# Two-operand matmuls 512 columns wide in the gate, up and down projections, and the normed activations moved by 32 bytes in SBUF

## The reference

```python
h   = rmsnorm(x, mix_norm_w);  u = h @ w_in            # forgetting attention and Mamba-2 SSD from u
x   = x + concat(y_A, y_B) @ w_out
h   = rmsnorm(x, ffn_norm_w)
g, up = split(h @ w_gate_up)                           # 2048 -> 2 * 5632
g   = causal_dwconv3(g)
x   = x + (silu(g) * up) @ w_down                      # 5632 -> 2048
h   = rmsnorm(x, ple_norm_w)
x   = x + sigmoid(h @ w_ple_gate) * (p @ w_ple_proj)
out = rmsnorm(x, final_norm_w)
```

## Time and profile before

| | us |
|---|---|
| median of 3 runs (1280.76 to 1281.69) | 1280.86 |
| the profiled execution: its time / its span | 1281.42 / 1279.7 |
| TensorE busy / weight loads busy (they overlap) | 1267.1 / 1221.7 |
| VectorE / ScalarE / GpSimd busy | 829.0 / 604.4 / 60.7 |
| DMA | 177 GB/s, 58% of the 16 engines' span |

### The profile page before, as it was taken

One profiled execution on the slowest core, in us unless ns is written; L12 is line 12 of the kernel. 1 busy time (PEld: TensorE's weight loads), 2 busy tenths in 40 slices (PEclk: granted clock), 3 DMA queues, 4 the chain that ended last, 5 costly groups with the idle time before them and its releaser, 6 DMA issues.

```text
span 1279.7 us, 25047 instructions
## 1 busy us (share of the span) xinstructions
PE 1267.1 (99%) x9950; PEld 1221.7 (95%) x9950; DVE 829.0 (65%) x1068; ACT 604.4 (47%) x775; POOL 60.7 (5%) x66
## 2 busy tenths in 40 slices
PE   9999999999999999999999999999999999999997
PEld 7999998789999999999999999999999999999885
DVE  6698777777777576665665575666665464646554
ACT  6444555556544454444444444443444343434555
POOL 2000000001221100000000000000001010101000
PEclk9999999999999999999999999999999999999998
DMA  8566555435556566666666666666655656566652
GB/s 257 160 188 186 155 148 148 116 114 151 186 176 198 181 182 182 182 182 184 183 184 182 180 180 181 181 181 183 188 183 167 209 162 208 165 211 204 196 188 99
DMA packets 118020, 227.05 MB, mean 177 GB/s; under 512 B 7392, under 2 KB 8452, under 8 KB 117828
## 3 DMA queue, kind: packets, MB, share of 16 engines
q1 hardware_dynamic: 117860, 225.89, 58.0%
q0 software_dynamic: 96, 0.26, 0.1%
HBM read 224.03 MB, written 2.10 MB: 177 GB/s over the span
## 4 chain that ended last, share of the span: by engine, by line
PE 98%; DMA 1%; SPq 0%; ACT 0%; issue 0%; DVE 0%; ACTq 0%; DVEq 0%
PE ps L316 27%; PE ps L317 27%; PE ps L318 27%; PE ps L343 4%; PE ps L345 4%; PE ps L344 4%; DMA w_raw<-in_w_in 1%; PE ps L734 1%; PE ps L737 1%; PE ps L778 1%; PE ps L761 0%; PE ps L791 0%; PE ps L748 0%; PE ps L776 0%; PE ps L902 0%
## 5 line engine op out<-in xcount | busy, mean ns | idle before, releaser
L301 DVE TENSOR_TENSOR w_lo<-w_raw,w_hi 128x1024 fp32r<-128x1024 f32 x413 | 506.4, 1231 | 366.6 <-ACT w_hi L296 363.8
L296 ACT ACTIVATE w_hi<-w_raw 128x1024 fp32r<-128x1024 f32 x413 | 435.9, 1058 | 525.3 <-PE ps L318 484.8
L316 PE MATMUL ps<-hHi,w_hi 128*128 128x256 f32 x1984 | 564.5, 285 | 0.8 <-DVE w_lo L301 0.8
L317 PE MATMUL ps<-hLo,w_hi 128*128 128x256 f32 x1984 | 561.3, 283 | 0.0
L318 PE MATMUL ps<-hHi,w_lo 128*128 128x256 f32 x1984 | 561.3, 283 | 0.0
L316 PEld LDWEIGHTS ps<-hHi,w_hi 128*128 128x128 f32 x1984 | 380.2, 192 | 1.5 <-issue 1.4
L317 PEld LDWEIGHTS ps<-hLo,w_hi 128*128 128x128 f32 x1984 | 380.3, 192 | 0.0
L318 PEld LDWEIGHTS ps<-hHi,w_lo 128*128 128x128 f32 x1984 | 380.2, 192 | 0.0
L316 PE MATMUL ps<-actHi,w_hi 128*128 (+1 forms) x704 | 196.9, 280 | 0.0
L317 PE MATMUL ps<-actLo,w_hi 128*128 (+1 forms) x704 | 196.9, 280 | 0.0
L318 PE MATMUL ps<-actHi,w_lo 128*128 (+1 forms) x704 | 196.9, 280 | 0.0
(11 more groups left out here) (242 smaller groups left out, 969.5 us busy)
## 6 DMA issues: line engine op xcount, KB each, us to landing
w_raw<-in_w_gate_up SPq DMA_DIRECT2D x176, 512.0 KB, 4.0
w_raw<-in_w_in SPq DMA_DIRECT2D x88, 512.0 KB, 3.7
w_raw<-in_w_down SPq DMA_DIRECT2D x88, 512.0 KB, 4.8
w_raw<-in_w_out SPq DMA_DIRECT2D x32, 512.0 KB, 4.7
w_raw<-in_w_ple_gate SPq DMA_DIRECT2D x32, 512.0 KB, 4.7
w_raw<-in_w_ple_proj SPq DMA_DIRECT2D x4, 512.0 KB, 5.4
out_x<-out_tok SPq DMA_DIRECT2D x8, 256.0 KB, 3.1
xtok<-in_x SPq DMA_DIRECT2D x3, 512.0 KB, 8.8
```

Of the source, the lines that this page charges most:

```text
L296: act.activation(parts(n)[0], w_raw[:, n % RING, :], ACT.Copy).then_inc(w_hi_made, 1)
L301: dve.tensor_tensor(lo, w_raw[:, n % RING, :], hi, ALU.subtract).then_inc(w_lo_made, 1)
L316: pe.matmul(dst, hi, opHi(k), start=start and m % 2 == 0, stop=False, skip_group_check=True)
L317: pe.matmul(dst, hi, opLo(k), start=False, stop=False, skip_group_check=True)
```

## The change

- `multiply_wide`: the activation's hi and lo parts now lie side by side (`h_parts`, `act_parts`: 512 columns for each k). One matmul of 512 columns multiplies `w_hi` by both, w_hi·xHi into columns 0 to 255 of a bank and w_hi·xLo into columns 256 to 511; one of 256 columns adds w_lo·xHi to the second half. Each 128-wide output tile now fills a bank, so a step over 512 weight columns takes 4 banks instead of 2 and the two halves of PSUM hold one unit each.
- The gate and up chunks are cut otherwise: two k slices by 256 gate and 256 up columns, 8 chunks to a unit, in two DMAs of 128x512 each, in runs of 256 columns of memory (1 KB) instead of 512 (2 KB). Still 176 chunks of 512 KB.
- The two halves of a bank have to be added. ScalarE copies the second half to `sumsq` and `sq` (`ffn_unit_part`), VectorE adds, then scales by `rms` in two ops of their own; `add_down` adds each half to `xT`, 4 ops for 2.
- `STATS1_AT` goes from chunk 11 to chunk 4 of the first 8-chunk unit.
- 32 bytes of padding ahead of `h_parts` and 32 behind. In the built program `h_parts` begins 32 bytes past a multiple of 128; `w_raw`, `w_hi` and `w_lo` 64 past; the arena 96 past; `pHi` at a multiple of 128. So the distance of the arena's tiles from the weight tiles is what it was, that of h from them is now 32 bytes more or less than a multiple of 64.
- The in-projection and the token-wise groups keep their instructions and read h from `h_parts`.

```diff
-        hHi, hLo = sb("hHi", [P, KD, T], F32R), sb("hLo", [P, KD, T], F32R)
+        half_line = sb("half_line", [P, 8])
+        h_parts = sb("h_parts", [P, KD, 2, T], F32R)
+        line_rest = sb("line_rest", [P, 8])
+        hHi, hLo = h_parts[:, :, 0, :], h_parts[:, :, 1, :]
...
+        act_parts = at("act_parts", [P, FT, 2, T], F32R, 0)
+        actHi, actLo = act_parts[:, :, 0, :], act_parts[:, :, 1, :]
...
+        def load_unit_chunk(sp, n, src, q=0):
...
+            for a in range(2):
+                sp.dma_start(w_raw[:, n % RING, a * COLS:(a + 1) * COLS].rearrange("p (b c) -> p b c", b=2),
+                             src[:, a, :, :]).then_inc(w_landed[n % RING], 16)
...
+        def multiply_wide(pe, n, both_of, bank_of, first, last, q=0):
+
+            pe.wait_ge(w_lo_made, n + RING * q + 1)
+            for i in range(2 * MT):
+                k, m = divmod(i, MT)
+                both = both_of(k)
+                hi, lo = (w[:, n % RING, i * P:(i + 1) * P] for w in (w_hi, w_lo))
+                pe.matmul(ps[:, bank_of[m], :], hi, both.rearrange("p b t -> p (b t)"),
+                          start=first and k == 0, stop=False, skip_group_check=True)
+                mm = pe.matmul(ps[:, bank_of[m], T:2 * T], lo, both[:, 0, :],
+                               start=False, stop=last and k == 1, skip_group_check=True)
+            return mm.then_inc(w_used, 1)
...
-        STATS1_AT = 11
-        UNIT_AT = (3, 9)
+        STATS1_AT = 4
+        U_IN, U_TAPS, U_SILU, U_ACT, U_HI, U_LO = LEAD, LEAD + 1, LEAD + 2, LEAD + 3, LEAD + 4, LEAD + 4
...
+            def ffn_unit_part(u, half, unit_end):
+
+                act.wait_ge(w_used, unit_end)
+                act.wait_ge(ffn_out, u + 1)
+                for part, a in ((sumsq, 0), (sq, 2)):
+                    b = WIDE_BANKS[half][a]
+                    copy(part[:, :, :], ps[:, b:b + 2, T:2 * T]).then_inc(ffn_part, 1)
...
+            def add_down(g):
+
+                banks = WIDE_BANKS[g % 2]
+                for half in range(2):
+                    for b in range(2):
+                        k = MT * g + 2 * b
+                        part = ps[:, banks[2 * b]:banks[2 * b] + 2, half * T:(half + 1) * T]
...
+                        dve.tensor_tensor(xT[:, k:k + 2, :], part, xT[:, k:k + 2, :],
+                                          ALU.add).then_inc(x_new if half else x_part, 1)
```

More of the change, by code:

```diff
@@ L290, in make_hi @@
         def make_hi(act, n, q=0):
-            act.wait_ge(w_landed[n % RING], 16 * (n // RING + q + 1))
+            act.wait_ge(*landed(n, q))
             if RING <= n < n_last:
@@ L846, in ffn_chunk @@
             def ffn_chunk(n, k, half, q=0):
[L847 to L862, removed]
+                return multiply_wide(pe, n, lambda kk: h_parts[:, 2 * k + kk, :, :], WIDE_BANKS[half], k == 0, k == KU - 1, q)
+            for j in range(2):
+                for k in range(KU):
+                    if j == 0:
+                        if k == 0:
+                            for name in ("o1", "o2"):
+                                pe.wait_ge(*evacuated[name])
+                        pe.wait_ge(h_lo_made, KD + 2 * k + 2)
+                    elif k == 0:
+                        pe.wait_ge(root_made, 2)
+                        pe.wait_ge(*evacuated["o3"])
+                    ffn_chunk(n_ffn + j * KU + k, k, j)
+                    if j == 0 and k == STATS1_AT:
+                        pe.wait_ge(*evacuated["o0"])
+                        stats(1, 4, columns=False)
+            with pe.Fori(0, NU // 2 - 1) as i:
                 for j in range(2):
-                    for k in range(KD):
+                    for k in range(KU):
                         if k == 0:
-                            pe.wait_ge(ffn_out, i * 4 + (1, 3)[j])
-                        ffn_chunk(n_ffn + (1 + j) * KD + k, k, 1 - j, i * (2 * KD // RING))
+                            pe.wait_ge(ffn_out, i * 2 + (2 + j))
+                        ffn_chunk(n_ffn + (2 + j) * KU + k, k, j, i * (2 * KU // RING))
             for g in range(NDN):
@@ L1103, in ffn_unit_hi, with ffn_steps @@
                 copy(dst, gate_out[:, :, :]).then_inc(ffn_hi, 1)
-            with act.Fori(0, NG // 2) as i:
-                for j in range(2):
[L1107 to L1112, removed]
-                                ffn_unit_hi(i * 4 + (2 * j + b))
+            def ffn_steps(k, u, half, unit_end):
+                if k == U_IN:
+                    ffn_unit_part(u, half, unit_end)
+                if k == U_SILU:
+                    ffn_unit_silu(u)
+                if k == U_HI:
+                    ffn_unit_hi(u)
+            for j in range(2):
+                for k in range(KU):
+                    make_hi(act, n_ffn + j * KU + k)
+                    if j == 0:
+                        run(act_after, n_ffn + k, steps)
+                        if k == LEAD:
+                            leave_out(NDN - 1)
+                        if k == STATS1_AT + LEAD:
+                            stats(1, 4)
+                    else:
+                        ffn_steps(k, 0, 0, n_ffn + KU)
+            with act.Fori(0, NU // 2 - 1) as i:
+                for j in range(2):
+                    for k in range(KU):
+                        make_hi(act, n_ffn + (2 + j) * KU + k, i * (2 * KU // RING))
+                        ffn_steps(k, i * 2 + (1 + j), 1 - j, i * (2 * KU) + (n_ffn + (2 + j) * KU))
             for g in range(NDN):
                 n0 = n_down + g * KDN
-                peeled = 18 if g == 0 else 6
+                peeled = 10 if g == 0 else 6
                 for c in range(peeled):
@@ L1508, in _ @@
                 run(dve_after, n, steps)
-            for k in range(KD):
-                make_lo(dve, n_ffn + k)
-                run(dve_after, n_ffn + k, steps)
-                if k == LEAD:
-                    leave_out(NDN - 1)
-                    dve.memset(gate_in[:, :, :, 0:4], 0.0).then_inc(ffn_out, 1)
-                if k == STATS1_AT + LEAD:
-                    stats(1)
             def ffn_unit_conv(u, half, b):
@@ L1570, in _, with ffn_steps @@
-            with dve.Fori(0, NG // 2) as i:
+            def ffn_steps(k, u, half, unit_end):
+                if k == U_IN:
+                    dve.wait_ge(w_used, unit_end)
+                    ffn_unit_conv(u, half, half)
+                if k == U_TAPS:
+                    ffn_unit_taps(u, half)
+                if k == U_ACT:
+                    ffn_unit_act(u, half)
+                if k == U_LO:
+                    ffn_unit_lo(u)
+            for j in range(2):
+                for k in range(KU):
+                    make_lo(dve, n_ffn + j * KU + k)
+                    if j == 0:
+                        run(dve_after, n_ffn + k, steps)
+                        if k == LEAD:
+                            leave_out(NDN - 1)
+                            dve.memset(gate_in[:, :, :, 0:4], 0.0).then_inc(ffn_out, 1)
+                        if k == STATS1_AT + LEAD:
+                            stats(1)
+                    else:
+                        ffn_steps(k, 0, 0, n_ffn + KU)
```

125 lines of the change are left out of this document (62 added, 63 removed).

## The result

| | before | after |
|---|---|---|
| median of 4 runs each (lowest to highest), us | 1281.05 (1280.76 to 1281.69) | 1260.44 (1260.3 to 1261.09) |
| ratio, with its 95% interval | | 0.9839 (0.9822 to 0.9856) |
| profiled execution: time / span, us | 1281.42 / 1279.7 | 1260.39 / 1258.6 |

The change makes the kernel 20.6 us faster. Forecast were 1267 us and a range of 1249 to 1281.

A forecast was written before the change was run, and what follows sets the result against it. The prediction took TensorE's matmul rhythm as the bound. Its terms were 1281.4 - 12.7 - 0.5 - 4.7 + 3.3 + 0.5 = 1267.3 us for the profiled run, with the median 0.6 below: 1267, range 1249 to 1281.

The forecast's parts named there:

- What bounds it: Whole kernel: TensorE, busy 1267.1 of 1279.7 us at full clock; a change is worth what it does to its rhythm.
- The wide pair: Gate and up: 360.3 to 351.3 ns a tile, 12.7 us less; down: 352.0 to 351.3, 0.5 us less.
- the first rival: Gate, up, down: long matmul keeps its in-step 227.1 ns, pair 344.4; 28.7 us less, 1252 us; chance 0.22.
- The shift for the in-projection: In-projection: 1728 matmuls of 256 columns go from 120.0 to 117.3 ns, 4.7 us less.
- The token-wise groups: v and the ring's part of the gate groups: 480 matmuls from 227.1 to 234.0 ns, 3.3 us more.
- Doubled adds: Down groups: four adds for two delay the fifth w_lo; 0 to 0.3 us at four places, 0.5 us more.
- Evacuation, norm, DMAs: Gate and up: added VectorE and ScalarE ops, the earlier norm sum and 176 more DMA issues all stay hidden, costing nothing.
- No gain from the pair: Gate, up, down: the pair is no cheaper than its columns and the shift does nothing; 1281 us; chance 0.07.
- The pair at the higher rate, slower: Gate, up, down: alternating widths cost 360.3 ns a pair, 4.9 us more, 1286 us; decides from 358.0 ns; chance 0.13.
- A wait that takes over: Each unit: w_lo or a landing more than 3 chunks late, each us of it costing 22; chance 0.08.

The follow-up runs named there:

- experiment 2: The changed kernel without the two 32-byte paddings, so h is in step with the weight ring: 1261.01 us, 0.9841 of before.
- experiment 4: The changed kernel with 96 bytes of padding behind h instead of 32, weight ring back at a multiple of 128 bytes: 1260.44 us, 0.9838 of before.
- experiment 5: The kernel before with seven extra short float32 matmuls in the down projection, addresses of everything else as before: 1284.18 us (one run).
- experiment 3: The kernel before with only the two 32-byte paddings around h: 1275.14 us, 0.9955 of before.
- experiment 7: The changed kernel with a down group's split (make_h) moved behind the next two w_lo on VectorE and w_hi on ScalarE: 1259.65 us, 0.9832 of before.
- experiment 1: The changed kernel with each wide matmul split into two of 256 columns, all else of the change kept: 1275.6 us, 0.9959 of before.
- experiment 6: The changed kernel with seven extra short float32 matmuls in its down projection: 1262.56 us (one run).

## Why the prediction was right, and where not

*What bounds it.* Right: TensorE's rhythm, at the full clock, with waits for weights of 1.1 us in 1258.6. The gain is all in the spacing of matmuls, as said.

*The wide pair.* The mechanism was right, the size was not, and this is the step that failed: "I take the value at 32 off since address is what the rows sort by". The pair was taken at 351.3 ns and is 347.2 and 347.1 as the mean of its two stages, inside its bounds of 344.4 and 360.3; undisturbed it is 346.7 with h in step (experiment 2), 32 short and 32 past (experiment 4). The rows in step nearly give it when they are read as a price per matmul and one per column: the earlier trace rows have 120.1 for 256 columns, 227.1 for 512, so 107.0 ns for 256 columns and 13.1 for each matmul. A tile has three times the former; three narrow ones add 3 x 13.1, in all 360.3, a pair 2 x 13.1, in all 347.2. That was the first rival's mechanism ("what is paid is per matmul"), and only its narrow part was taken at 117.3 instead of 120.1. The 4.1 ns too much make 1408 x 4.1 = 5.8 us in gate and up, the 4.2 in down 3.0. Together they are more than the error of the forecast, 6.6 us; errors of the other sign, below, took off the rest, and that is luck.

The account per matmul fits the narrow rows at 120 and the pair. It isn't shown as a rule: narrow rows at 118.3 and 117.3 and long ones at 233 have other remainders over their columns, and no run shows why.

The Trainium skill (TensorE: Matmul & The Clock Gate, Back-to-back issue gap) gives 2.5 ns beyond the columns for an isolated matmul, and says that this counts too little for short ones in a stream where each brings its weight load. This kernel is such a stream, and its trace agrees with that: 256 columns take 10.6 to 13.3 ns beyond their 106.7 at 2.4 GHz. Of long matmuls the section says that the figure counts too much, and there the trace disagrees: 512 columns take 13.4 to 20.7 ns beyond their 213.3. The whole change by 2.5 ns a matmul, an estimate of 5.3 us, is a quarter of the 20.6 measured.

*The shift for the in-projection.* Half right. Over 40 us of it the change has 338 matmuls and the kernel before 333, by windows of TensorE, first before, then after:

```profile
60.00:100.00 40.00, 40.00 (x333) 1.00 0.60 182
```

```profile
60.00:100.00 40.00, 40.00 (x338) 1.00 0.61 177
```

That is 1.5% less, 118.3 ns and not 117.3: 1728 x 1.7 = 2.9 us for the 4.7 predicted. The step that failed here took 32 bytes short and 32 bytes past for one distance; with weights 128 columns wide, 117.3 had been read at the latter alone. And the address alone does not fix the rate: 117.3, 118.7 and 120.0 all occur at one and the same set of addresses (experiments 4 and 5). The shift is one of the things that change the rate, a break is another.

*What the step didn't have.* The out-projection, 768 narrow matmuls whose tiles kept their distance from the weights, lost 1.03 us, from 117.3 to 118.7. It was costed at nothing because of its addresses, by the same error.

*The token-wise groups.* Right for the gate groups. They go to 233 or 234 as the earlier trace rows, also those that were at 227.1 in the earlier trace rows (timeline of TensorE, after, 23 steps in 5.37 us):

```profile
1191.55 0.39 PE L374 MATMUL ps<-w_hi,h_parts 128*128 128x512 f32 x1
...
1196.92 0.40 PE L376 MATMUL ps<-w_hi,h_parts 128*128 128x512 f32 x1
```

The stage behind down is 2.14 us longer, of which 288 x 6.3 = 1.8 are these; the shift alone (experiment 3) makes it 1.8 longer. For v the price of before was misread. Its 192 matmuls weren't at 227.1 but at 228.5 to 230.8 (as in a row of 11 from 223.74 to 226.05 us, 231 each), and they are at 233 after: 192 x 2.6 = 0.5 us for the 1.3 predicted.

*Doubled adds.* Right in mechanism, 0.7 us by experiment 7 for the 0.5 predicted (half a microsecond by the last stage of experiments 1 and 3, 114.72 and 114.22 us); most of it at one place, behind `dn3`, where the group that follows has matmuls of 512 columns.

*Evacuation, norm, DMAs.* Right: nothing. Experiments 1 and 3 have the same lengths for both stages.

*The rivals.* No gain from the pair: refuted, it is worth 15 to 20 us. The pair at the higher rate, slower: refuted, since in gate and up all pairs but the first 39 and those at the norm are at 346.7, and the 39 at 353.2, still under the 358.0 that would decide for it. But what it rests on is real: a slower rhythm of pairs exists, and narrow matmuls can fall to 120.0 where they stood at 117.3. A wait that takes over: none. The first rival came nearer in mechanism (a matmul fewer is the gain) and further off in time (1252), since it gave the remaining narrow one a rate of 117.3 and all the other terms as forecast.

*The sum.* Terms found, in us: pair and narrow rate in gate and up -18.5, in down -3.8, in-projection about -2.9, out-projection +1.0, token-wise groups about +2.3, adds +0.7. Together -21.2, of 21.1 measured. The stretch up to the out-projection can't be read finer than about 1 us: with h in step it was 321.6 us before, 322.9 in experiment 2 and 321.1 in experiment 5.

## What to carry to other kernels

When TensorE is the bound and its matmuls are short, price a matmul as so much per column plus so much per instruction, both from the kernel's own rows of two widths at the same place, and count what falls away. What it brings depends on the rate that the narrow ones had: here each matmul less was worth 13.1 ns where they stood at 120, 8.1 at 118.3 and 4.9 at 117.3. Don't explain a rate of 117 against 120 ns by whatever tells two stages apart until one run has changed that alone: the address sorted five stages well and was half of the key. Read a rate over a whole stage as well as in one stretch, since a short matmul in between can end one rhythm and begin another. And a gain of such a shift on narrow matmuls (5.8 us here) may be gone (0.6) once they are wide, so measure such edits on top of each other.

## What the runs showed of the hardware

- A row of 128x128 by 256 matmuls, float32r, each with new weights, at the full clock: with the moving tile in step with the weights 120.0 ns, 32 bytes short of them 118.3 as a mean over long stretches, 32 past them 117.3, 118.7 or 120.0. In the last case a short matmul in between can move it from one to another and back at the same addresses: 117.3, 118.7, 118.7, 118.6, 117.3, 118.7, 117.3, 120.0 in the eight stretches of experiment 5.
- Rows of 512 and 256 columns in turn stand at 346.7 ns a pair at all three distances, and stay there behind seven breaks. A slower rhythm exists: 353 ns in the first 39 pairs of gate and up, until a norm's short matmuls, in the change and in experiments 2, 6 and 7, but not in experiment 4.
- Rows of 512 columns alone do show something like the address: 227.1 from the ring and 234.0 from `last_hi` before, 233 from both once h had moved. In experiment 4 the arena is in step with h and the ring is not, and it is turned round: the ring's at 233 (1222.83 to 1223.53 us, 3 steps), those of `last_hi` and `last_lo` at 227 (1229.35 to 1231.62, 10 steps).
- The Trainium skill (SBUF — State Buffer, Specifications) gives lines of 16 bytes, from which one would expect 32 bytes more to make no difference. The shift alone made this kernel 5.8 us faster.
- Open: what of the 13.1 ns is the weight load's and what the instruction's, since no run had a matmul that kept its weights; by what rule a break picks one of the rates, and why the first pairs of gate and up are slower.
